# Stacked depthwise taps in four column groups, with shifted rows copied through DRAM

## The reference, cut to what matters

```
mod = silu(c) @ w_mod[i] + b_mod[i]        # 6 vectors of 1024 for latents and context, from w_mod (1024 x 6144)
h   = modulate(rms_norm(x, norm1_g), mod[0], mod[1])
a, gate = split(h @ conv_w_pw1, 2)          # 1024 -> 2048
u   = a * sigmoid(gate)
u   = depthwise_conv(u, w_dw, 31 taps, padding 15) + b_dw
u   = silu(layer_norm(u, ln_g, ln_b))
x   = x + mod[2] * (u @ conv_w_pw2)
```

## Time and profile before

| | us |
|---|---|
| median of three runs (2343.87 to 2348.84) | 2348.62 |
| profiled execution | 2348.4 |
| its span, first to last instruction | 2346.1 |
| PE busy (TensorE matmul) | 2223.6 (95%) |
| DVE busy (VectorE) | 1417.1 (60%) |
| ACT busy (ScalarE) | 807.3 (34%) |
| POOL busy (GpSimd) | 667.5 (28%) |

### The profile page before, as it was taken

How to read it: one execution, slowest core, us unless ns; L and a number is a source line. 1 busy time by engine, 2 the same in 40 slices (tenths; PEclk the granted TensorE clock), 3 DMA queues, 4 the chain that set the end, 5 groups by cost and what they waited for, 6 DMA issues and landing times.

```text
span 2346.1 us, 30707 instructions
## 1 busy us (share of the span) xinstructions
PE 2223.6 (95%) x11666; PEld 1787.7 (76%) x11666; DVE 1417.1 (60%) x1872; ACT 807.3 (34%) x1145; POOL 667.5 (28%) x377
## 2 busy tenths in 40 slices
PE   6999969899999999998999999999997999899997
PEld 5677748788888888885457888887886888788885
DVE  5789982654444445544563754655418552699997
ACT  3212134211111111333663311111322543677775
POOL 0000014233333333431444344444542234011001
PEclk8999979999999999999999999999999999899999
DMA  9455532432222222220002233333232234599996
GB/s 309 156 160 169 198 124 81 179 138 63 63 63 63 63 63 63 66 72 10 10 1 64 83 98 92 97 98 113 72 90 63 63 76 153 188 394 403 406 405 252
DMA packets 248208, 312.12 MB, mean 133 GB/s; under 512 B 13642, under 2 KB 199595, under 8 KB 235827
## 3 DMA queue, kind: packets, MB, share of 16 engines
q1 hardware_dynamic: 236764, 275.33, 34.8%
q0 software_dynamic: 6688, 25.69, 2.8%
q10 hardware_dynamic: 4663, 9.79, 1.1%
HBM read 286.13 MB, written 24.65 MB: 132 GB/s over the span
## 4 chain that ended last, share of the span: by engine, by line
PE 84%; DVE 10%; ACT 2%; POOL 1%; DMA 1%; issue 1%; DVEq 0%; POOLq 0%; SPq 0%; ACTq 0%
PE acc L609 48%; PE acc L3013 8%; PE pb L3031 4%; PE acc L2524 3%; PE acc L2735 2%; PE pa L2749 2%; PE pb L2470 2%; PE pb L2762 2%; PE acc L661 2%; PE acc L643 2%; PE acc L2588 1%; DVE csum L1748 1%; DVE hid_hi L1813 1%; PE acc L690 1%; PE pa L2410 1%
## 5 line engine op out<-in xcount | busy, mean ns | idle before, releaser
L548 POOL TENSOR_TENSOR wlo<-raw,whi 128x1024 fp32r<-128x1024 f32 x180 | 449.5, 2498 | 907.1 <-ACT whi L537 887.0
L537 ACT ACTIVATE whi<-raw 128x1024 fp32r<-128x1024 f32 x188 | 198.4, 1059 | 890.3 <-PE acc L609 836.1
L609 PE MATMUL acc<-ah,whi 128*128 128x256 f32 (+1 forms) x1256 | 393.7, 362 | 5.0 <-DVE sg L2008 2.6
L609 PE MATMUL acc<-al,whi 128*128 128x256 f32 (+1 forms) x1256 | 389.4, 359 | 0.0
L609 PE MATMUL acc<-ah,wlo 128*128 128x256 f32 (+1 forms) x1256 | 388.9, 358 | 0.0
L609 PEld LDWEIGHTS acc<-ah,whi 128*128 128x128 f32 x1256 | 235.6, 189 | 48.3 <-issue 8.9
L609 PEld LDWEIGHTS acc<-ah,wlo 128*128 128x128 f32 x1256 | 236.7, 188 | 36.8
L609 PEld LDWEIGHTS acc<-al,whi 128*128 128x128 f32 x1256 | 236.7, 188 | 36.1 <-issue 0.5
L1833 DVE SCALAR_TENSOR_TENSOR x<-acc,mod,x 128x512 f32<-128x512 f32 (+1 forms) x174 | 109.7, 658 | 232.2 <-PE acc L609 232.1
L1037 DVE TENSOR_TENSOR expert_lo<-expert_pair,expert_hi 128x1024 fp32r<-128x1024 f32 x192 | 224.5, 1219 | 14.5 <-ACT expert_hi L1032 14.5
L1032 ACT ACTIVATE expert_hi<-expert_pair 128x1024 fp32r<-128x1024 f32 x192 | 201.4, 1059 | 63.4 <-PE acc L3013 40.1
(11 more groups left out here) (501 smaller groups left out, 3684.4 us busy)
## 6 DMA issues: line engine op xcount, KB each, us to landing
raw<-in_w_ff SPq DMA_DIRECT2D x128, 512.0 KB, 4.0
mod_raw<-in_w_mod SPq DMA_DIRECT2D x80, 512.0 KB, 5.8
expert_pair<-in_expert_w_gate SPq DMA_DIRECT2D x32, 1024.0 KB, 8.0
expert_pair<-in_expert_w_up SPq DMA_DIRECT2D x32, 1024.0 KB, 7.7
expert_pair<-in_expert_w_down SPq DMA_DIRECT2D x32, 1024.0 KB, 7.3
raw<-in_w_in SPq DMA_DIRECT2D x30, 512.0 KB, 3.8
raw<-in_conv_w_pw SPq DMA_DIRECT2D x24, 512.0 KB, 8.8
expert_rows_dram<-zero_rows POOLq DMA_DIRECT2D x1, 12288.0 KB, 38.1
```

Source lines behind the costliest of these rows:

```text
L537: e.eng.activation(whi[e.n["q"] % 2][:, :], raw[r][:, :], ACT.Copy).then_inc(S["hi_ready"], 1)
L548: e.eng.tensor_tensor(wlo[b][:, :], raw[e.n["g"] % RING][:, :], whi[b][:, :].bitcast(F32), ALU.subtract).then_inc(S["lo_ready"], 1)
L609: ins = e.eng.matmul(o, w, m, start=keys.index(key) == n, stop=len(keys) - 1 - keys[::-1].index(key) == n)
```

## The change

- PE's taps become 12 in tiles 0 to 5, 16 in tile 6 and 24 in tile 7 (`TAP_BLOCKS` of 4 shifts each; tile 0 had none). A block multiplies 128 rows, which are 4 shifts times 32 channels, with 32 columns of `tap_rows`, once for each of four groups of 32 channels, and writes that group's partitions of `pbk`: per block 4 matmuls over 512 and 4 over 271 columns.
- For this the rows of `upb` must lie shifted on the partitions: SP writes `upb` (416 KB) to DRAM, waits for it, and reads it back with four transfers of 32 partitions x 4 x `width` into `shifted`, one for each shift (`stack_rows`). It stands in SP's order after the tile's second chunk (in the last tile after the third).
- POOL makes `tap_rows` (`place_taps`) in place of ACT's diagonals, and it makes the low halves of the weight slabs of this stage in place of DVE.
- DVE does 19 taps in tiles 0 to 5, 15 in tile 6 and 7 in tile 7, adds PE's sum at tap `SUMS_AT`, and gates the next tile at tap `GATE_AT`.
- PE's order in tile i of 0 to 6: chunk, taps of tile i-1, turn, projection, chunk, projection, turn. Taps of tile 6 follow, and those of tile 7 stand before chunk 21.
- Six more constant transfers on ACT's queue bring the tap weights in the stacked order.

```diff
-PE_TAPS = (0, 6, 6, 6, 6, 6, 6, 9)
+TAP_BLOCKS = (3, 3, 3, 3, 3, 3, 4, 6)
+GATE_AT = (16, 10, 10, 10, 10, 10, 10)
+SUMS_AT = (18, 15, 15, 15, 15, 15, 13, 6)
...
-    diag = sb("diag", [P, max(PE_TAPS), P], at=h_at + 16384)
+    tap_rows = [sb(f"tap_rows{b}", [P, max(TAP_BLOCKS[b::2]), P], at=h_at + 16384 + 2048 * b) for b in range(2)]
+    shifted = sb("shifted", [P, 4, PAD + CTX + PAD + LAT + 6], at=e_at)
...
+        def stack_rows(i):
+            sp.wait_ge(S["glu_done"], i + 1)
+            if i:
+                sp.wait_ge(S["shifted_in"], 64 * i)
+            sp.dma_start(u_t.ap(), upb[i % 2][:, :]).then_inc(S["gated_out"], 16)
+            sp.wait_ge(S["gated_out"], 16 * (i + 1))
+            if i:
+                sp.wait_ge(S["conv_summed"], i)
+            width = wide + SHIFTS * (TAP_BLOCKS[i] - 1)
+            for n in range(SHIFTS):
+                sp.dma_start(shifted[32 * n:32 * n + 32, :, 0:width],
+                             bass.AP(u_t, by_vector(i) + n, [[u_rows, 32], [32 * u_rows, 4], [1, width]])
+                             ).then_inc(S["shifted_in"], 16)
...
         for i in range(KT):
-            for n in CHUNKS_OF_TILE[i]:
+            mod_load(e, CHUNKS_OF_TILE[i][0])
+            load_pw(4 + 2 * i)
+            load_pw(5 + 2 * i)
+            for n in CHUNKS_OF_TILE[i][1:3]:
                 mod_load(e, n)
-                if n == CHUNKS_OF_TILE[i][0]:
-                    load_pw(4 + 2 * i)
-                    load_pw(5 + 2 * i)
+            stack_rows(i)
+            for n in CHUNKS_OF_TILE[i][3:]:
+                mod_load(e, n)
...
+        for b in range(4):
+            rows_of_taps(32 * b, 3, TAP_SPLIT + SHIFTS * b, range(KT))
+        rows_of_taps(88, 1, 11, range(KT))
+        rows_of_taps(120, 1, 7, (KT - 1,))
...
+        def place_taps(i):
+            if i >= 2:
+                pool.wait_ge(S["conv_summed"], i - 1)
+            for j in range(TAP_BLOCKS[i]):
+                ins = pool.tensor_tensor(tap_rows[i % 2][:, j, :].rearrange("p (g c) -> p g c", g=4),
+                                         mod_pick[:, :].unsqueeze(1).to_broadcast([P, 4, 32]),
+                                         stacked_taps(by_vector(i) + SHIFTS * j, i).unsqueeze(2).to_broadcast([P, 4, 32]),
+                                         ALU.mult)
+            ins.then_inc(S["diag_ready"], 1)
+        place_taps(0)
+        place_taps(1)
+        for i in range(1, KT - 1):
+            split_first(e, split_low)
+            split_first(e, split_low)
+            if i < KT - 1:
+                place_taps(i + 1)
+            add_tile(i - 1)
+        add_tile(KT - 2)
...
-            for t in range(2, by_vector):
-                if t == late:
+            for t in range(2, by_vector(i)):
+                if t == SUMS_AT[i]:
...
-                if t in beside:
-                    beside[t]()
+                if i < KT - 1 and t == GATE_AT[i]:
+                    gated(i + 1)
+                    tile_modulation(i)
...
         def conv_taps(i):
-            pe.wait_ge(S["glu_done"], i + 1)
-            pe.wait_ge(S["diag_ready"], i)
+            pe.wait_ge(S["shifted_in"], 64 * (i + 1))
+            pe.wait_ge(S["diag_ready"], i + 1)
+            if i:
+                pe.wait_ge(S["conv_taken"], i)
+            count = TAP_BLOCKS[i]
+            for c0, c1 in ((0, 512), (512, wide)):
+                for j in range(count):
+                    for g in range(4):
+                        part = slice(32 * g, 32 * g + 32)
+                        ins = pe.matmul(pbk[part, c0:c1], tap_rows[i % 2][:, j, part],
+                                        shifted[:, g, SHIFTS * j + c0:SHIFTS * j + c1], start=j == 0, stop=j == count - 1)
...
+        for i in range(KT - 1):
             first, second = CHUNKS_OF_TILE[i]
-            mod_chunk(first, pa[:, 0:512], after_product=i > 1)
-            conv_taps(i)
+            mod_chunk(first, pa[:, 0:512], after_product=True)
+            if i:
+                conv_taps(i - 1)
             pe.wait_ge(S["mod_added"], first)
             turn_mod(first, turned_at(i, first))
+            project(2 * i + 2)
             mod_chunk(second, pa[:, 0:512])
-            project(2 * i + 2)
+            project(2 * i + 3)
             turn_mod(second, turned_at(i, second))
-            project(2 * i + 3)
-        conv_taps(KT - 1)
+        conv_taps(KT - 2)
         pe.wait_ge(S["acc_free"], e.at("u", 2))
         for n in LAST_CHUNKS:
+            if n == LAST_CHUNKS[-1]:
+                conv_taps(KT - 1)
```

More of the change, by code:

```diff
@@ L493, in tap_sources, with by_vector, stacked_taps @@
         return ((taps[i % 2][:, 0:TAP_SPLIT], cols[:, C_TAP_A:C_TAP_A + 8 * TAP_SPLIT], column(i)),
-                (taps[i % 2][:, TAP_SPLIT:TAPS], cols[:, C_TAP_B:C_TAP_B + 8 * (TAPS - TAP_SPLIT)], column(i)))
+                (taps[i % 2][:, TAP_SPLIT:TAP_SPLIT + SHIFTS], cols[:, C_MORE_TAPS:C_MORE_TAPS + 8 * SHIFTS], column(i)))
+    def by_vector(i):
+        return TAPS - SHIFTS * TAP_BLOCKS[i]
+    def stacked_taps(first, i):
+        at = {11: C_VEC + 88 + 4 * i, 7: C_VEC + 120}.get(first, 384 + 8 * (first - TAP_SPLIT) + 4 * i)
+        return cols[:, at:at + 4]
     def chunk_at(n):
@@ L1235, in take_taps @@
             act.activation(taps[i % 2][:, TAPS:TAPS + 1], cols[:, bias:bias + 1], ACT.Copy).then_inc(S["taps_ready"], 1)
-        def make_diagonals(i):
-            act.wait_ge(S["taps_ready"], i + 1)
-            if i >= 2:
-                act.wait_ge(S["conv_summed"], i - 1)
-            for j in range(PE_TAPS[i]):
-                t = TAPS - PE_TAPS[i] + j
-                ins = act.activation(diag[:, j, :], mats[:, M_ID, :], ACT.Copy, scale=taps[i % 2][:, t:t + 1])
-            ins.then_inc(S["diag_ready"], 1)
         take_taps(0)
@@ L1669, in _ @@
         dve.wait_ge(S["vec_turned"], 1)
-        for n, rows in enumerate((96, 88, 120, 128)):
+        for n, rows in enumerate((128, 124, 120, 128)):
             ins = dve.tensor_copy(cols[:, P * n:P * n + rows], pbk[:, P * n:P * n + rows])
@@ L1719, in conv_tile @@
             here, part = upb[i % 2], taps[i % 2]
-            by_vector = TAPS - PE_TAPS[i]
-            beside = {}
-            if i < KT - 1:
-                beside[17 if i == 0 else 12] = lambda: (gated(i + 1), tile_modulation(i))
-            if i < KT - 2:
-                for t in (20, 22):
-                    beside[t] = lambda: split_first(e, split_low)
             dve.wait_ge(S["taps_ready"], i + 1)
@@ L1729, in conv_tile @@
                 dve.wait_ge(S["cv_ready"], i)
-            late = 6 if i == KT - 1 else None
-            if PE_TAPS[i] and not late:
-                dve.wait_ge(S["conv_summed"], i)
-                STT(out=csum[1][:, :], in0=here[:, 1:1 + wide], scalar=part[:, 1:2], in1=pbk[:, 0:wide],
-                    op0=ALU.mult, op1=ALU.add).then_inc(S["conv_taken"], 1)
-                dve.wait_ge(S["conv_taken"], i)
-                e.step(TS(csum[0][:, :], here[:, 0:wide], part[:, 0:1], part[:, TAPS:TAPS + 1], ALU.mult, ALU.add))
-            else:
-                TS(csum[1][:, :], here[:, 1:1 + wide], part[:, 1:2], None, ALU.mult)
-                e.step(TS(csum[0][:, :], here[:, 0:wide], part[:, 0:1], part[:, TAPS:TAPS + 1], ALU.mult, ALU.add))
-            for t in range(2, by_vector):
-                if t == late:
+            TS(csum[1][:, :], here[:, 1:1 + wide], part[:, 1:2], None, ALU.mult)
+            e.step(TS(csum[0][:, :], here[:, 0:wide], part[:, 0:1], part[:, TAPS:TAPS + 1], ALU.mult, ALU.add))
+            for t in range(2, by_vector(i)):
+                if t == SUMS_AT[i]:
                     dve.wait_ge(S["dve_chain"], e.at("c"))
-                    dve.wait_ge(S["conv_summed"], i)
+                    dve.wait_ge(S["conv_summed"], i + 1)
                     TT(csum[0][:, :], csum[0][:, :], pbk[:, 0:wide], ALU.add).then_inc(S["conv_taken"], 1)
-                    dve.wait_ge(S["conv_taken"], i)
+                    dve.wait_ge(S["conv_taken"], i + 1)
                 if t > 3:
@@ L2392, in _ @@
             turn_tokens(b)
-        pe.wait_ge(S["consts_in"], 16 * 12)
-        for n, rows in enumerate((96, 88, 120, 128)):
+        pe.wait_ge(S["consts_in"], 16 * 18)
+        for n, rows in enumerate((128, 124, 120, 128)):
             ins = pe.transpose(pbk[:, P * n:P * n + rows], vec_rows[0:rows, n, :], ident[0:rows, 0:rows])
```

55 lines of the change are left out of this document (22 added, 33 removed).

## The result

Five executions of the changed kernel took 2324.32 to 2335.25 us, median 2330.69; five of the kernel before 2343.87 to 2351.21, median 2348.62. The ratio is 0.9927 (95% interval 0.9904 to 0.9949). The kernel got faster by 18 us, half of the 35.3 that I had forecast (2313.0), and the time lies above my range of 2304 to 2328. The profiled execution took 2335.25 us, its span 2333.4.

A forecast was written before the change was run, and what follows sets the result against it. PE bounds the tile period, DVE's last tile the end. Of 35.3 us gained, 9.5 come by the period from 129.57, 21.6 from five later periods, 5.2 from the tail, less 2 for lag: 2348.4 - 35.3 = 2313.1, 80% range 2304 to 2328.

The forecast's parts named there:

- Which views, and what bounds the kernel: Convolution stage: PE sets the tile period (busy 30.71 of 30.88 us), DVE's last tile sets the end.
- Start: Kernel start: six more constant transfers cost 0, range 0 to 3 us; after tile 0 the next period starts at 93.6.
- Taps and period: Middle tiles on PE: taps 4.0 us in place of 8.01, period 26.45 us in place of 30.88.
- The rival of column groups that overlap less: PE's taps: column groups overlap less at 271 columns, 5.3 in place of 4.0 us, costing 12 us, 2325; chance 8%.
- Vector and POOL: Middle tiles: DVE (Vector) and POOL exclude each other, DVE's cycle 27.5 us, 1 us over PE's; cost 2, range 0 to 6.
- the 2 us of allowance: Middle tiles: loss allowed for DVE falling behind PE, range 0 to 6 us, putting the last projection's end at T = 253.4.
- the rival not in force: Middle tiles: DVE and POOL set the period, six periods losing 5 to 6 us in place of 2; 2318 if bad; chance 20%.
- "Cost 0" for the copies in the middle tiles: Middle tiles: DRAM write lands near +9.5, reads near +13, PE wants them at +28.3; next chunk's load has 4 us margin.
- the +18.5: Time in a period past which the copy chain decides, 7 us later than expected; kernel slower from 13 us later on.
- my fourth rival: Middle tiles: copies hold the SP queue, cycle 35 us, 51 us more, 2364, slower than before; chance 6%.
- The end of the stage: Last tile: DRAM chain sets the end; write T+15, rows T+19.6, taps to T+27.5, centring T+37.3 = 290.7, with 1 us for clock.
- The rival of a clock that stays up: Tail and norm: PE's clock stays up, mean and spreading matmuls giving 3 to 5 us back, 2309; chance 7%.

The follow-up runs named there:

- again: The changed kernel once more, nothing edited; median 2330.21 us, ratio to before 0.9916.
- quarter: Changed kernel with reads of a quarter of the columns (100 KB each) in tiles 1 to 7; 2312.45 us profiled, one execution.
- once: Changed kernel with the copies run for tile 0 alone, PE using those shifted rows for every tile; median 2314.91 us, ratio to before 0.9849.
- via4: Changed kernel with each read bringing one column group to all 128 partitions, channels outermost (row 4 * channel + shift); median 2322.58 us, ratio to before 0.9890.
- rows128: Changed kernel with each read taking the same 128 source rows but going to all 128 partitions, rows not stacked; 2316.97 us profiled, one execution.
- direct_order: via4's layout copied SBUF to SBUF without the DRAM write; last tile's rows between chunks 19 and 20 on SP and PE; median 2319.43 us, ratio to before 0.9857.
- direct_order5: direct_order with 20 taps in place of 24 on PE in the last tile; median 2318.41 us, ratio to before 0.9850.
- via_order5: via4's copies through DRAM in direct_order's last-tile order, write ahead of chunk 19, 20 taps on PE there; median 2316.30 us, ratio to before 0.9851.

## Why the forecast was wrong, step by step

**Which views, and what bounds the kernel: right.** PE set the period before and sets it now, Vector's last tile set the end of the stage.

**Start: right.** PE waits 0.76 us for the constants (1.62 in again), within my 0 to 3. The start of period 1 lay between 93.6 and 96.8 in the executions with periods like the changed kernel's; I had 93.6. In again, as in quarter, it is 2.0 later with a granted clock of 0.61 in 76 to 79 us, a term that my sum did not have.

**Taps and period: right.** 4.06 us (4.0) and 26.53 (26.45). The rival of column groups that overlap less is refuted, and so are the 5.2 us that the prediction worked out from the 3.07x of the page "TensorE: Matmul & The Clock Gate", section "Measured speedup vs the span model", of the Trainium skill.

**Vector and POOL: half right.** They exclude one another, as four steps of 8.04 us show, and POOL's work is longer than I had (10.53 us a tile, not 7.9). Vector is busy 25.82 us of a period, where I had a cycle of 27.5, so no lag builds up; the 2 us of allowance were not needed. The six clean periods of once, with POOL's work in place, show the rival not in force.

**"Cost 0" for the copies in the middle tiles: wrong, and this is the failed step.** I took the four reads for 104 KB each, the size of 32 rows of `upb`. A read fills 32 partitions, but with four groups: 32 x 4 x 791 x 4 bytes = 400 KB, as the diff says. Four are 1.6 MB, not 0.4, and into 32 partitions they go at 200 GB/s. They are issued 13.5 us into the period (107.17), since the write ahead of them lands 4 us later than the +9.5 that I had (10.6 to 12.0 us into the period even in quarter), and run until some 116.5, 23 us into it, in place of landing at +13. So the copy chain passes the +18.5 that the prediction had named as the point where it decides; the next chunk, whose load I had given 4 us of margin, comes late by 0.3 and costs 1.4. What came is the mechanism of my fourth rival, the copies that hold SP's queue, at a small part of its price. Four of six periods: T at 257.85, where clean periods from 93.64 end at 251.9. That is 5.9 us, of which the unused 2 us for Vector hid a part (4.4 net); in again three late periods cost 3.4 us, behind the later start. The size did not do this alone: with all 1.6 MB but 128 target partitions T is 254.4 and 254.9 (via4, rows128), so in the middle tiles it took the 200 GB/s as well.

**The end of the stage: right in kind, wrong by the same term.** Write landed T+17.2 (15), rows T+27.2 (19.6): of 7.6 us, 2.2 lie with the write behind a full queue (1.7 remain in quarter, so they are not the size; that it takes 1 us for its data and 1 us to the semaphore is a split that no run shows) and 5.4 with reads of four times the size. Behind the rows 17.1 us (17.7): the clock cost 1.5 us in the taps (2.5 in again) where I had put 1, and what follows the taps takes 7.7 (8.8). Net 7.0. Together 11.4 us, the whole miss of the centring; quarter takes the size alone away and lands at 289.96. The rival of a clock that stays up did not come: the granted clock is 0.58 in 302 to 321.

**From the centring to the time.** The forecast added my gain to a profiled execution with the short MLP. The profiled one after had the long one, and so had an unknown part of the five: like against like the change is worth 22 to 23 us, and 2348.4 - 22.4 = 2326. The other 5 us between that and 2330.69 are, as far as is known, this difference between executions: the traces show it for profiled executions alone, and how many of the others had the longer MLP stays open. The trace of before could not show it by itself, and no range of mine contained it. Even so 2326 would have stood near the upper end of the range. (The 1 us that the prediction's sum leaves to rounding is the turn: it stands behind the last projection now, and stood ahead of it before.)

## What to carry to other kernels

Work out the bytes of each transfer from its target's shape (partitions x everything behind them), and compare the sum per period with what the queue moves in it: here 7.0 MB (263 GB/s for 26.53 us), of which 1.6 at half rate, with DMA busy for 0.92 of the period. A replicating copy costs its target's bytes, not its source's. Let a transfer reach all 128 partitions and look at the slowest dimension of both sides: with 32 or 128 there, the same 1.6 MB ran into 128 partitions at some 300 GB/s (some 400 behind a chunk), at 200 into 32 partitions, and at some 85 with 4 as the slowest dimension of the source. And when an experiment hits the forecast, compare the terms too: quarter's 0.8 us hid six errors of 1 to 2 us.

## What the runs showed of the hardware

- Transfers from SBUF to SBUF ran at some 200 GB/s behind a chunk (8.2 us for 1.6 MB in direct_order and in direct_order5), reads from DRAM into the same layout at some 400 (4.1 us, via_order5). Each direct transfer reads out of 32 partitions only, and 32 partitions on the target side ran at 200 too; whether SBUF as a source or its 32 partitions set the rate, no run parts. GB/s of direct_order, 250 to 300 us; the rows are the slices from 124 to 226:

```profile
GB/s 408 403 341 290 287 221 377 421 387 303 124 141 203 221 272 170 190 226 261 280 333 405 392 408 392 365 231 98 0 0 0 118 354 400 400 377 30 0 13 0
```

- Float32 matmuls of one and the same program ran at a pitch of 0.3467 or 0.3533 us (482.56 and 491.83 us for 2784 records, two each), through the whole MLP at the full granted clock. What decides it stayed open; all sixteen profiles had one or the other.
- An issue on SP took 5.27 us in place of 0.3 to 0.4 where 4 MB stood in its queue (260.01 in the profile after), and 2.6 to 2.7 at the same place in via4, rows128 and quarter.
